# Zeroing the expert row table during the dense up stage, and forming the gate third of the last adaLN set behind the routing sums

## The chip, the cores and the metric

The kernel runs on one core of a Trainium2 chip. The metric is device time in microseconds (us), lower is better, taken as the median of several runs. The engines are TensorE (PE, with its weight loads as PEld), VectorE (DVE), ScalarE (ACT), GpSimd (POOL) and SyncE (SP), each with its own instruction queue; they meet only at semaphores. SP issues the weight loads, POOL issues the transfers of the expert rows, and all of them run on the same 16 DMA engines.

## The reference, cut to what matters

One inference step of a two-layer decoder on 256 prompt tokens and 8 sample tokens, width 1024, float32. Layer 1 ends in a mixture of experts behind an adaLN modulation:

```python
sh, sc, gt = ada_mod(c, ada_ffn_w[1], ada_ffn_b[1])    # (silu(c) @ w + b), split in three
hf = rms_norm(x, g_pre_ffn[1]) * (1.0 + sc) + sh
logits = hf @ w_router + b_router
top_v, top_i = lax.top_k(logits, 2); gates = softmax(top_v)
f = sum over e of dense_gate[:, e] * swiglu(hf, w1[e], w3[e], w2[e])
x = x + gt * rms_norm(f, g_post_ffn[1])
```

The thirds sh and sc of the set are needed before the router sees hf. The third gt is needed only for the last line.

## The kernel before

Tokens stand in columns (264 of them) and features in partitions, in 8 blocks of 128. Weights stream in as slabs of 1 MB through `ring`, which has 7 slots; SP issues the load of a slab when its slot is free. Every weight product but the adaLN ones is made in three passes over a high and a low part of the operands (lines 474 to 476): ACT writes the high part of a slab to `w_hi`, DVE the low part to `w_lo`.

**The adaLN sets.** Four sets, each 12 slabs of 4 x 128 rows and 512 columns, two slabs for each of 6 blocks `j` of columns. `ada_product(s, j)` (line 525) multiplies the nine conditioning vectors, which stand in columns 0 to 8 of `c32`, by two slabs; ACT copies the result (`ada_rows`, line 1015) to `arow`, and `ada_columns` (line 511) turns it into columns of bank 6, where DVE's `ada_take` (lines 1388 to 1391) adds the bias and folds the norm's gains in. Blocks 0 to 3 are sh and sc, blocks 4 and 5 are gt. A ring slot that holds an adaLN slab is free as soon as its product is done (`ada_used`).

**The last set and the routing**, the stage that the change touches, in the order of each engine:

- PE: the six products of set 3 with two norm sums in between (`norm_sum`, line 536), the logits (`logit_strips`, line 838: `c32` now holds the router's weights in columns 0 to 7), the transposes of hf to token rows (`token_rows`, line 846), the sum of the strips by `fold` (856), the positions in each expert (866), the loads (871), 8 triples of transposes of x (877), 8 transposes of the gate third (880), one count matmul (883), the gate rows spread over the tokens (888 and 889), the transposed picks (893), and then, once the rows of expert 0 are in (`x_in`) and the gate rows are out (`gate_taken`), the transposes of those rows (904) and the first expert.
- ACT: `ada_rows`, the norm's squares and roots, the router weights into `c32` (1251 and 1252), the high parts of the first three expert slabs (1262), the token rows out of PSUM (1268, 1269), the softmax exponent (1272), the rows of x out of PSUM (1276, 1277).
- DVE: the norm (1400, 1404), four small operations, `ada_take`, `modulate` (1413 to 1415), then the routing arithmetic up to the row numbers (1772), the gates, the picks (1797), and the gate rows (1801, 1806, 1807).
- POOL: after the output projection is out of PSUM (`wo_taken`) it sets `ye` to zero (1936) and writes it over the 8 slabs of the expert row table `x_rows` in DRAM (`clear`, 8 transfers of 512 KB, line 1945). Later it scatters the 264 token rows twice into that table (6 indirect transfers, 1950) and loads the slab of expert 0 (1986). Each expert takes 128 slots, so rows that no token fills have to be zero.
- SP: the 12 slabs of set 3 and behind them, without a break, those of expert 0. Expert slab k goes into the slot of adaLN slab 5 + k for k up to 6, and from slab 7 on a slot is free when DVE has written `w_lo` of the slab seven before.

Then 8 experts follow, 42 slabs each.

Of the kernel before, what the change touches and what calls it, by code (L numbers as in the profile page):

```python
# [12 lines left out]
P = 128  # L13
D = 1024
# [25 lines left out]
NEG = -1e30  # L40

# [56 lines left out]
def yoco_step(nc, w, o):  # L98
# [25 lines left out]
    with ExitStack() as ctx:  # L124
# [62 lines left out]
        rb = sb("rb", [NE, 1])  # L187
# [102 lines left out]
        rb_strip = at(11904, 1)  # L290
# [177 lines left out]
        def _(pe):  # L468
# [46 lines left out]
            def ada_product(s, j):  # L515
# [12 lines left out]
                if j >= 1:  # L528
                    ada_columns(s, j - 1)
# [294 lines left out]
            for j in range(6):  # L824
                ada_product(3, j)
                if j == 0:
                    norm_sum(5)
                if j == 2:
                    norm_sum(6)
            ada_columns(3, 5)  # L830


            def logit_strips(hf):

                pe.wait_ge(rw_spread, 1)
# [19 lines left out]
            for c, n in ((0, P), (1, P), (2, NB)):  # L855
                mm = pe.matmul(bank[0][0:n, NE * c:NE * (c + 1)], std[:, P * c:P * c + n], fold[:, 0:NE], start=True, stop=True)
# [15 lines left out]
            mm.then_inc(load_summed, 1)  # L872
            for k in range(KC):
                if k >= 2:
# [109 lines left out]
        def _(act):  # L984
# [128 lines left out]
            i_lin, i_wo = firsts[("wq", 0)], firsts[("wo", 0)]  # L1113
            highs(i_lin + 1)
# [127 lines left out]
            for j in range(6):  # L1242
# [30 lines left out]
            ins.then_inc(lg_exp, 1)  # L1273
            for k in range(KC):
# [66 lines left out]
        def _(dve):  # L1341
# [10 lines left out]
            dve.tensor_reduce(fold[:, :], ident.rearrange("p (a b) -> p b a", a=4)[:, 0:9, :], X, ALU.add).then_inc(fold_ready, 1)  # L1352
            dve.tensor_reduce(cst("head"), ident.rearrange("p (a r) -> p r a", a=8), X, ALU.add)
# [27 lines left out]
            def ada_take(s, kind, layer):  # L1381

                a = ada[:, s]
                dve.wait_ge(ada_turned, 6 * (s + 1))
# [3 lines left out]
                link(dve.tensor_tensor(a, sums, across(vec1[:, col:col + 24], 9), ALU.add))  # L1388
# [699 lines left out]
```

## Time and profile before

| | us |
|---|---|
| median of 3 runs (lowest, highest) | 1695.52 (1694.08, 1696.55) |
| span of the profiled execution | 1693.5 |
| busy: PE, PEld | 1587.1, 1295.9 |
| busy: DVE, ACT, POOL | 1255.3, 982.6, 153.9 |
| from the first product of set 3 to the first expert matmul | 638.55 to 713.13 |
| the 8 experts | 713.13 to 1672.8 |

The times are of whole executions. For the profiled execution only its span is given; the median of the runs is 2.0 us above that span, which is what lies around it. "Granted clock" in the tables of stretches is TensorE's clock as a share of 2.4 GHz: 0.50 is 1.2 GHz, 1.00 is 2.4 GHz, and a value between is a stretch in which it changed. A matmul of float32 shows as two instructions in the trace, so a product of 8 matmuls is "x16" there. Matmuls overlap, so the start of the next row says more than the length of one.

### The profile page before, as it was taken

How to read it: one execution, taken by the hardware profiler on the slowest of the kernel's cores; microseconds unless marked ns; L12 is line 12 of the kernel's file. 1: busy time of each engine (PE TensorE's matmuls, PEld its weight loads, DVE VectorE, ACT ScalarE, POOL GpSimd, SP SyncE). 2: the span in 40 equal slices, each digit the busy share in tenths (PEclk: the TensorE clock that was granted, in tenths of full speed). 3: DMA queues.
4: the chain of work that ended last, by engine and by line, in shares of the span. 5: the costliest groups of instructions: out<-in, count | busy, mean ns of one | idle time of the engine just before them, and what ended most of it. 6: DMA issues, size and time to landing. Idle time of an engine off the chain costs nothing.

```text
span 1693.5 us, 22933 instructions
## 1 busy us (share of the span) xinstructions
PE 1587.1 (94%) x8697; PEld 1295.9 (77%) x8697; DVE 1255.3 (74%) x1097; ACT 982.6 (58%) x885; POOL 153.9 (9%) x135
## 2 busy tenths in 40 slices
PE   6889999799899887899999999999999999999996
PEld 3579999498785574488888888888888888888874
DVE  4355543578782834488898888988888888889996
ACT  2244432433322633277777877877877877777774
POOL 0000000025541511200000000000000000000210
PEclk9789999899999988599999999999999999999998
DMA  9895555855458428689999999999999999999991
GB/s 345 295 346 177 180 160 183 299 174 194 155 212 305 141 75 333 214 320 382 359 389 384 355 395 364 380 387 379 370 391 367 378 386 364 382 386 363 394 386 49
DMA packets 248254, 512.28 MB, mean 302 GB/s; under 512 B 9046, under 2 KB 68614, under 8 KB 248176
## 3 DMA queue, kind: packets, MB, share of 16 engines
q1 hardware_dynamic: 241015, 490.27, 80.6%
q0 software_dynamic: 4768, 16.89, 2.5%
q10 hardware_dynamic: 2400, 4.17, 0.7%
q8 instruction: 45, 0.74, 0.2%
q14 instruction: 26, 0.21, 0.0%
HBM read 498.19 MB, written 13.82 MB: 302 GB/s over the span
## 4 chain that ended last, share of the span: by engine, by line
PE 76%; DVE 9%; DMA 5%; POOL 3%; ACT 3%; issue 3%; SPq 1%; DVEq 0%; ACTq 0%; POOLq 0%
PE wide L474 22%; PE wide L475 22%; PE wide L476 22%; DVE w_lo L1729 2%; POOL phase L1907 2%; DMA ring<-in_ada_mix_w 2%; DVE phase L1570 2%; DMA ring<-in_ada_ffn_w 1%; PE wide L930 1%; POOL phase L1913 1%; ACT w_hi L1262 1%; PE wide L525 1%; PE wide L536 1%; SPq L437 1%; DMA ring<-in_cache_v 1%
## 5 line engine op out<-in xcount | busy, mean ns | idle before, releaser
L1729 DVE TENSOR_TENSOR w_lo<-ring,w_hi 128x2048 fp32r<-128x2048 f32 x336 | 767.6, 2290 | 114.0 <-ACT w_hi L1262 112.5
L1262 ACT ACTIVATE w_hi<-ring 128x2048 fp32r<-128x2048 f32 x336 | 643.6, 1919 | 216.5 <-PE wide L476 214.3
L474 PE MATMUL wide<-w_hi,xe_hi 128*128 128x512 f32 x896 | 355.7, 397 | 5.6 <-DVE w_lo L1729 2.9
L475 PE MATMUL wide<-w_lo,xe_hi 128*128 128x512 f32 x896 | 350.2, 391 | 0.0
L476 PE MATMUL wide<-w_hi,xe_lo 128*128 128x512 f32 x896 | 350.2, 391 | 0.0
L474 PE MATMUL wide<-tHi,w_hi 128*128 128x264 f32 x672 | 198.3, 295 | 20.4 <-DVE mLo L1488 20.4
L404 DVE TENSOR_TENSOR w_lo<-ring,w_hi 128x2048 fp32r<-128x2048 f32 (+1 forms) x58 | 139.0, 2399 | 101.2 <-ACT w_hi L1002 100.9
L475 PE MATMUL wide<-mLo,w_hi 128*128 128x264 f32 x736 | 212.3, 288 | 0.0
L474 PEld LDWEIGHTS wide<-w_hi,xe_hi 128*128 128x128 f32 x896 | 169.0, 189 | 45.1 <-DVE w_lo L1729 8.6
L476 PEld LDWEIGHTS wide<-w_hi,xe_lo 128*128 128x128 f32 x896 | 168.8, 188 | 35.8
L475 PEld LDWEIGHTS wide<-w_lo,xe_hi 128*128 128x128 f32 x896 | 169.0, 189 | 33.4
L476 PE MATMUL wide<-tHi,w_lo 128*128 128x264 f32 x672 | 192.9, 287 | 0.0
L474 PE MATMUL wide<-w_hi,upT_hi 128*128 128x512 f32 x448 | 177.1, 395 | 0.0
L475 PE MATMUL wide<-w_lo,upT_hi 128*128 128x512 f32 x448 | 176.2, 393 | 0.0
L476 PE MATMUL wide<-w_hi,upT_lo 128*128 128x512 f32 x448 | 174.2, 389 | 0.0
L474 PEld LDWEIGHTS wide<-tHi,w_hi 128*128 128x128 f32 x672 | 129.3, 192 | 30.2 <-issue 29.9
L1002 ACT ACTIVATE w_hi<-ring 128x2048 fp32r<-128x2048 f32 (+1 forms) x58 | 109.1, 1885 | 61.2 <-PE wide L476 61.1
L475 PEld LDWEIGHTS wide<-mLo,w_hi 128*128 128x128 f32 x736 | 142.1, 193 | 0.3
L476 PEld LDWEIGHTS wide<-tHi,w_lo 128*128 128x128 f32 x672 | 129.0, 192 | 0.0
L476 PEld LDWEIGHTS wide<-w_hi,upT_lo 128*128 128x128 f32 x448 | 84.1, 188 | 19.0
L474 PEld LDWEIGHTS wide<-w_hi,upT_hi 128*128 128x128 f32 x448 | 84.1, 188 | 18.5
L475 PEld LDWEIGHTS wide<-w_lo,upT_hi 128*128 128x128 f32 x448 | 84.3, 188 | 16.5
(313 smaller groups left out, 1709.8 us busy)
## 6 DMA issues: line engine op xcount, KB each, us to landing
ring<-in_moe_w SPq DMA_DIRECT2D x336, 1024.0 KB, 7.4
ring<-in_ffn_w SPq DMA_DIRECT2D x30, 1024.0 KB, 5.4
ring<-in_ada_mix_w SPq DMA_DIRECT2D x24, 1024.0 KB, 8.8
ring<-in_ada_ffn_w SPq DMA_DIRECT2D x24, 1024.0 KB, 12.0
ring<-in_w_q SPq DMA_DIRECT2D x12, 1024.0 KB, 9.1
ring<-in_cache_k SPq DMA_DIRECT2D x24, 512.0 KB, 4.9
ring<-in_cache_v SPq DMA_DIRECT2D x24, 512.0 KB, 6.3
ring<-in_w_kv SPq DMA_DIRECT2D x8, 1024.0 KB, 6.5
```

Of the source, the lines that this page charges most:

```text
L404: eng.tensor_tensor(w_lo[:, i % PAIRS, 0:size], ring[:, n % RING, 0:size], w_hi[:, i % PAIRS, 0:size].bitcast(F32), ALU.subtract).then_inc ...
L437: sp.dma_start(slab_view(n), slab_source(item)).then_inc(slab_in[n % RING], 16)
L474: pe.matmul(out, a[0], b[0], start=start, stop=False, skip_group_check=True)
L475: pe.matmul(out, a[0], b[1], start=False, stop=False, skip_group_check=True)
L476: return pe.matmul(out, a[1], b[0], start=False, stop=stop, skip_group_check=True)
L525: mm = pe.matmul(out[32 * k:32 * (k + 1), :], c32[:, 4 * half + k, :], slab_view(n)[:, k, :], start=(half == 0), stop=(half == 1))
L536: mm = pe.matmul(bank[7][:, 0:NT], ones, tT[:, k, :], start=(k == 0), stop=(k == KC - 1))
L1002: act.activation(w_hi[:, i % PAIRS, 0:size], ring[:, n % RING, 0:size], ACT.Copy).then_inc(hi_done, 1)
L1262: act.activation(w_hi[:, (NSPLIT + k) % PAIRS, :], ring[:, slot, :], ACT.Copy).then_inc(hi_done, 1)
L1570: ins = dve.tensor_tensor(k_prod[t % 2][:, cols], slab_view(n)[:, t % 2, cols], bank[6 + q], ALU.mult)
L1729: dve.tensor_tensor(w_lo[:, i, :], ring[:, slot, :], w_hi[:, i, :].bitcast(F32), ALU.subtract).then_inc(lo_done, 1)
L1907: pool.tensor_tensor(out, rawT[:, r % 4, :], cos, ALU.mult).then_inc(cos_done, 1)
```

## The change

Two things are done, and a third follows from them.

1. **Zeroing.** POOL no longer waits for the output projection. Behind its three small loads in the up stage of the dense feed-forward (the router's weights and bias, and cos and sin) it waits until both halves of the operand's low part are written (`act_lo`), sets the first 1024 columns of `hT` to zero and issues the 8 transfers from there. DVE, before it writes `hT` again (`gated(1, mT)`), waits for all 8 to have landed.
2. **The gate third.** Of set 3, PE, ACT and DVE do blocks 0 to 3 in the old place. The products of blocks 4 and 5 stand behind the loads (line 879 and 880 of the new kernel), their columns behind the first two of the 8 triples of transposes of x, and DVE's share behind the picks. The count matmul moves ahead of the gate's transposes, because DVE writes the gate third only after the picks, which need the count.
3. **The router's weights** must now be in `c32` together with the conditioning vectors. They go to columns 16 to 23, once, right after set 2; `fold_r` is the sum matrix for those columns, and the router's bias stands in partitions 16 to 23 of `rb`, in place of `rb_strip`.

```diff
             pe.wait_ge(wo_taken, KC)
-            for j in range(6):
+            pe.wait_ge(rw_spread, 1)
+            for j in range(4):
                 ada_product(3, j)
...
-            ada_columns(3, 5)
+            ada_columns(3, 3)
...
             mm.then_inc(load_summed, 1)
+            pe.wait_ge(ht_taken, KC)
+            ada_product(3, 4, columns=False)
+            ada_product(3, 5, columns=False)
             for k in range(KC):
+                if k == 2:
+                    ada_columns(3, 4)
+                    ada_columns(3, 5)
                 if k >= 2:
                     pe.wait_ge(x2_taken, k - 1)
...
+            pe.wait_ge(arow_ready, 6 * 3 + 5)
+            pe.matmul(bank[2][:, 0:P], ones, before, start=True, stop=True).then_inc(count_row, 1)
+            pe.wait_ge(ada_taken, 5)
             for k in range(KC):
                 mm = pe.transpose(bank[6 + k // 4][0:1 + NB, P * (k % 4):P * (k % 4 + 1)], ada[:, 3, 16 + k, :], ident)
             mm.then_inc(gate_turned, 1)
-            pe.wait_ge(ht_taken, KC)
-            pe.matmul(bank[2][:, 0:P], ones, before, start=True, stop=True).then_inc(count_row, 1)
...
+            act.wait_ge(ada_used, 36)
+            act.wait_ge(in_router, 32)
+            act.activation(c32[:, :, ROUTER:ROUTER + NE], rw[:, :, :], ACT.Copy).then_inc(rw_spread, 1)
             highs(i_lin + 1)
...
-            for j in range(6):
+            for j in range(4):
                 ada_rows(3, j)
...
-            act.wait_ge(ada_used, 48)
-            act.wait_ge(in_router, 32)
-            act.activation(c32[:, :, 0:NE], rw[:, :, :], ACT.Copy)
-            act.activation(c32[:, :, NE:NE + 1], c32[:, :, NE + 1:NE + 2], ACT.Copy).then_inc(rw_spread, 1)
...
             ins.then_inc(lg_exp, 1)
+            ada_rows(3, 4)
+            ada_rows(3, 5)
...
+            dve.wait_ge(cleared, 16 * NE)
             gated(1, mT)
...
-            ada_take(3, 1, 1)
+            ada_take(3, 1, 1, 0, 16)
...
             ins.then_inc(pick_ready, 1)
+            ada_take(3, 1, 1, 16, 24)
             dve.wait_ge(gate_turned, 1)
...
             pool.wait_ge(in_rope, 16)
+            pool.wait_ge(act_lo, 2)
+            pool.memset(hflat[:, 0:D], 0.0).then_inc(zero_ready, 1)
+            pool.wait_ge(zero_ready, 1)
...
+            clear(0, hflat[:, 0:D])
...
-            pool.wait_ge(wo_taken, KC)
-            pool.memset(ye[:, :], 0.0).then_inc(zero_ready, 1)
-            pool.wait_ge(zero_ready, 1)
...
-            clear(0)
             pool.wait_ge(cleared, 16 * NE)
             pool.wait_ge(ht_taken, KC)
             pool.wait_ge(row_ready, 1)
```

**PE at the end of set 3**, before. A row is a line of the kernel, the operation, its output and inputs and the output's shape, and in brackets the semaphores that it waits for; L525 is a product, L511 the columns, L838 the logits:

```order
L511 MATMUL wide<-fold,shared 128x9 [waits arow_ready]
L511 MATMUL wide<-fold,shared 128x9 x3
L525 MATMUL wide<-ring,c_60 32x512 [waits slab_in2,arow_ready]
L525 MATMUL wide<-ring,c_60 32x512 x3
L525 MATMUL wide<-ring,c_60 32x512 [waits slab_in3]
L525 MATMUL wide<-ring,c_60 32x512 x3
L511 MATMUL wide<-fold,shared 128x9 [waits arow_ready]
L511 MATMUL wide<-fold,shared 128x9 x3
L511 MATMUL wide<-fold,shared 128x9 [waits arow_ready]
L511 MATMUL wide<-fold,shared 128x9 x3
L838 MATMUL wide<-hT,c_60 32x264 [waits h_ready,rw_spread]
```

and in the changed kernel, where the same lines are 526, 512 and 839:

```order
L526 MATMUL wide<-ring,c_60 32x512 [waits slab_in5,arow_ready]
L526 MATMUL wide<-ring,c_60 32x512 x3
L526 MATMUL wide<-ring,c_60 32x512 [waits slab_in6]
L526 MATMUL wide<-ring,c_60 32x512 x3
L512 MATMUL wide<-fold,shared 128x9 [waits arow_ready]
L512 MATMUL wide<-fold,shared 128x9 x3
L512 MATMUL wide<-fold,shared 128x9 [waits arow_ready]
L512 MATMUL wide<-fold,shared 128x9 x3
L839 MATMUL wide<-hT,c_60 32x264 [waits h_ready]
L839 MATMUL wide<-hT,c_60 32x264 x3
```

The logits stood behind six pairs of slabs and now stand behind four; the last pair ahead of them is the one in ring slots 5 and 6.

**PE behind the loads**, before (L871 are the loads, L877 the transposes of x, a triple for each block k):

```order
L871 MATMUL wide<-phase,const 128x8 x3
L877 MATMUL wide<-const,xT 128x128 x2
L877 MATMUL wide<-const,xT 8x128
L877 MATMUL wide<-const,xT 128x128 x2
L877 MATMUL wide<-const,xT 8x128
L877 MATMUL wide<-const,xT 128x128 [waits x2_taken]
```

and now, where L872 are the loads, L884 the transposes of x and L512 the columns:

```order
L872 MATMUL wide<-phase,const 128x8 x3
L526 MATMUL wide<-ring,c_60 32x512 [waits slab_in0,arow_ready,ht_taken]
L526 MATMUL wide<-ring,c_60 32x512 x3
L526 MATMUL wide<-ring,c_60 32x512 [waits slab_in1]
L526 MATMUL wide<-ring,c_60 32x512 x3
L526 MATMUL wide<-ring,c_60 32x512 [waits slab_in2,arow_ready]
L526 MATMUL wide<-ring,c_60 32x512 x3
L526 MATMUL wide<-ring,c_60 32x512 [waits slab_in3]
L526 MATMUL wide<-ring,c_60 32x512 x3
L884 MATMUL wide<-const,xT 128x128 x2
L884 MATMUL wide<-const,xT 8x128
L884 MATMUL wide<-const,xT 128x128 x2
```

Four groups of four matmuls of 512 columns stand between the loads and the transposes of x; the first waits for the token rows to be out of PSUM (`ht_taken`). The columns of both blocks come behind the second triple.

**PE at the gate's transposes**, before (L880), with the count matmul (L883) behind them:

```order
L877 MATMUL wide<-const,xT 8x128
L880 MATMUL wide<-const,ada 9x128 x8
L883 MATMUL wide<-const 128x128 [waits ht_taken]
L888 MATMUL wide<-phase,mT 128x512 [waits x2_taken,gate_rows]
L889 MATMUL wide<-phase,const 8x512
```

and now, count matmul L887, gate's transposes L890:

```order
L884 MATMUL wide<-const,xT 8x128
L887 MATMUL wide<-const 128x128 [waits arow_ready]
L890 MATMUL wide<-const,ada 9x128 [waits ada_taken]
L890 MATMUL wide<-const,ada 9x128 x7
L896 MATMUL wide<-phase,mT 128x512 [waits x2_taken,gate_rows]
L897 MATMUL wide<-phase,const 8x512
```

The gate's transposes now wait for `ada_taken`, that is for DVE, which does its share behind the picks, which wait for the count matmul.

## Rows read from the trace of the kernel before

**Rows 1.** Chain that ended last, 610 to 725 us: start, length, what.
```profile
649.89 16.98 DMA ring<-in_ada_ffn_w
673.25 1.38 DVE hT L1413 x4
697.43 6.94 DMA x_rows<-phase,row
704.66 3.72 DMA hT<-x_rows
708.51 1.96 PE wide L904 x8
713.13 0.79 PE wide L474
```

**Rows 2.** Page, costliest groups: busy, mean ns, idle before and its releaser.
```profile
L474 PE MATMUL wide<-w_hi,xe_hi 128*128 128x512 f32 x896 | 355.7, 397 | 5.6 <-DVE w_lo L1729 2.9
```

**Rows 3.** Instructions in order of time, PE, 656 to 669 us: start, length.
```profile
656.91 1.92 PE L525 MATMUL wide<-ring,c 128*32 128x512 f32 x16
658.76 1.06 PE L511 MATMUL wide<-fold,shared 128*128 128x9 f32 x8
...
666.92 1.83 PE L525 MATMUL wide<-ring,c 128*32 128x512 f32 x8 [1.55 <-DMA ring<-in_ada_ffn_w]
668.68 3.58 PE L511 MATMUL wide<-fold,shared 128*128 128x9 f32 x16
```

**Rows 4.** Instructions in order of time, DVE, 659 to 673 us.
```profile
659.37 2.55 DVE L1404 TENSOR_TENSOR tT<-xT,rstd 128x1056 f32<-128x1056 f32 x2
...
662.13 0.15 DVE L1721 TENSOR_SCALAR phase<-const 128x8 f32<-128x8 f32 x1
...
672.30 0.38 DVE L1388 TENSOR_TENSOR ada<-wide,vec 128x216 f32<-128x216 f32 x1 [9.72 <-PE wide L511]
```

**Rows 5.** Stretches: busy of each engine, then granted clock, DMA share, GB/s.
```profile
655.00:660.00 5.00, 5.00 (x36) 2.91 (x40) 2.44 (x2) 1.08 (x2) 0.00 (x0) 1.00 1.04 417
670.00:675.00 5.00, 2.27 (x11) 2.17 (x11) 2.43 (x9) 3.49 (x2) 0.00 (x0) 0.50 1.05 388
```

**Rows 6.** DMA queues, 639 to 658 us: POOL's queue, packets, MB, share.
```profile
q0 software_dynamic: 963, 3.55, 45.8%
```

**Rows 7.** Instructions in order of time, PE, 685 to 708 us.
```profile
686.89 1.54 PE L877 MATMUL wide<-const,xT 128*128 128x128 f32 x6
688.82 4.59 PE L877 MATMUL wide<-const,xT 128*128 128x128 f32 x18 [0.39 <-ACT phase L1277]
693.20 1.62 PE L880 MATMUL wide<-const,ada 128*9 128x128 f32 x8
694.66 0.39 PE L883 MATMUL wide<-const 128*128 128x128 f32 x2
697.45 1.75 PE L888 MATMUL wide<-phase,mT 9*128 9x512 f32 x2 [2.40 <-DVE phase L1801]
```

**Rows 8.** Instructions in order of time, DVE, 695 to 708 us.
```profile
695.16 1.04 DVE L1797 TENSOR_SCALAR phase<-wide,phase 128x128 f32<-128x128 f32 x3 [0.91 <-PE wide L883]
696.12 1.27 DVE L1801 COPY phase<-wide 9x512 f32<-9x512 f32 x2
704.83 0.69 DVE L1806 COPY phase<-wide 128x512 f32<-128x512 f32 x1 [7.44 <-PE wide L889]
...
706.64 0.67 DVE L1807 COPY phase<-wide 8x512 f32<-8x512 f32 x1
```

**Rows 9.** Stretches of 1 us in which TensorE's clock stands or changes.
```profile
694.00:695.00 1.00, 1.00 (x8) 0.67 (x5) 0.22 (x2) 0.00 (x0) 0.69 (x2) 0.80 1.00 270
...
718.00:719.00 1.00, 1.00 (x5) 0.86 (x4) 0.00 (x0) 0.36 (x1) 0.00 (x0) 0.86 0.00 0
```

**Rows 10.** Instructions in order of time, POOL, up stage: its last small load.
```profile
119.84 0.58 POOL L1900 DMA_DIRECT2D const<-in_shape_constants  x1
```

**Rows 11.** A stretch of the up stage, columns as in Rows 5.
```profile
132.00:134.00 2.00, 2.00 (x19) 2.00 (x18) 0.78 (x1) 0.00 (x0) 0.00 (x0) 1.00 0.21 42
```

More of the change, by code:

```diff
@@ L40 @@
 NEG = -1e30
+ROUTER = 16
 CONST = {}
@@ L513, in ada_columns, with ada_product @@
                 mm.then_inc(ada_turned, 1)
-            def ada_product(s, j):
+            def ada_product(s, j, columns=True):
                 if 6 * s + j >= 2:
@@ L527, in ada_product @@
                     mm.then_inc(ada_used, 1)
-                if j >= 1:
+                if j >= 1 and columns:
                     ada_columns(s, j - 1)
@@ L855, in _ @@
             for c, n in ((0, P), (1, P), (2, NB)):
-                mm = pe.matmul(bank[0][0:n, NE * c:NE * (c + 1)], std[:, P * c:P * c + n], fold[:, 0:NE], start=True, stop=True)
+                mm = pe.matmul(bank[0][0:n, NE * c:NE * (c + 1)], std[:, P * c:P * c + n], fold_r[:, :], start=True, stop=True)
             mm.then_inc(lg_summed, 1)
@@ L1379, in across, with ada_take @@
                 return a.unsqueeze(2).to_broadcast(list(a.shape[:2]) + [n])
-            def ada_take(s, kind, layer):
+            def ada_take(s, kind, layer, lo=0, hi=24):
                 a = ada[:, s]
-                dve.wait_ge(ada_turned, 6 * (s + 1))
+                dve.wait_ge(ada_turned, 6 * s + hi // 4)
                 dve.wait_ge(vec_read, 1)
@@ L1898, in _, with slab_rows, clear @@
             pool.dma_start(rw[:, :, :], w["router_w"][0].rearrange("(k p) n -> p k n", p=P)).then_inc(in_router, 16)
-            pool.dma_start(rb[:, :], w["router_b"].rearrange("a n -> n a")).then_inc(in_router, 16)
+            pool.dma_start(rb[ROUTER:ROUTER + NE, :], w["router_b"].rearrange("a n -> n a")).then_inc(in_router, 16)
             pool.dma_start(const[:, 0:2 * NT], w["shape_constants"][:, 0:2 * NT]).then_inc(in_rope, 16)
             pool.wait_ge(in_rope, 16)
+            pool.wait_ge(act_lo, 2)
+            pool.memset(hflat[:, 0:D], 0.0).then_inc(zero_ready, 1)
+            pool.wait_ge(zero_ready, 1)
+            def slab_rows(table, e, c):
+                at = SLOTS * (e + NE * max(c - 1, 0))
+                return table[min(c, 1)][at:at + SLOTS, :]
+            def clear(c, zeros):
+                for e in range(NE):
+                    pool.dma_start(slab_rows(x_rows, e, c), zeros).then_inc(cleared, 16)
+            clear(0, hflat[:, 0:D])
             def turned_half(r):
@@ L1934, in _ @@
             pool.sem_inc(y_free, 1)
-            pool.wait_ge(wo_taken, KC)
-            pool.memset(ye[:, :], 0.0).then_inc(zero_ready, 1)
-            pool.wait_ge(zero_ready, 1)
-            def slab_rows(table, e, c):
-                at = SLOTS * (e + NE * max(c - 1, 0))
-                return table[min(c, 1)][at:at + SLOTS, :]
-            def clear(c):
-                for e in range(NE):
-                    pool.dma_start(slab_rows(x_rows, e, c), ye[:, :]).then_inc(cleared, 16)
             def scatter(over):
```

22 lines of the change are left out of this document (12 added, 10 removed).

## The prediction, made before the changed kernel ran

> **What bounds the kernel now.** I read three views, in this order. The page says who is late in the experts, where most of the time goes: the 896 matmuls of line 474 waited 5.6 us in all [rows 2]. TensorE is the bound there, the change touches nothing in it, and so what counts is when the first expert starts. The chain of waits, followed back from that start, shows what held it: a weight slab of set 3 that took 16.98 us to land, then `modulate`, the routing, the scatter of the token rows, the gather of expert 0's rows (landed at 708.38), and the transposes of those at 708.51 [rows 1]. The instructions in order of time show who would be next: DVE had put the last gate row out at 707.31 [rows 8]. So the gate's chain was 1.1 us short of being the bound, and the rows have only this much to gain before it takes over, unless it moves too. That makes this stage a race of two chains, and the change hurries one and lengthens the other.
>
> **Part by part.** All times are in the profiled execution (span 1693.5 us); the median of the runs lies 2.0 us higher.
>
> *The head of the stage.* The product of block 3 began at 656.91, the last one, of block 5, got its second slab only at 666.92 [rows 3]. With the blocks 4 and 5 gone, columns of block 2 end at 659.8, ACT needs 0.6 us beside them, and the columns of block 3 take 1.06 [rows 3]: done at 660.9. DVE is later: the norm ends at 661.92, its small operations at 662.28 [rows 4]; two of them go, which saves 0.2. `ada_take` took 0.95 us from 672.30 to `modulate` at 673.25 [rows 1, 4]; without the gate third I take 0.75. So `modulate` starts at 662.4 + 0.75 = 663.15, **10.1 us earlier**. The new bound here is the norm, not the slabs. How much faster the slabs land without the 4.2 MB of zeros is then worth nothing by itself: slabs 6 and 7 were in time before, too. I let the routing behind it shift as it is: TensorE has a gap between 660.9 and the logits, which come behind the first half of `modulate`; behind the like gap before, its clock stood at 0.50 in 670 to 675 [rows 5], and I expect it at half in the routing again.
>
> *The scatter and the gather.* Shifted by 10.1, the last scatter lands at 694.3 and expert 0's rows allow the transposes at 698.4. That is the ceiling: a gain of 10.1.
>
> *The gate's chain.* Loads end and the transposes of x begin at 686.89 [rows 7], now 676.8. From there:
> - Products of blocks 4 and 5, new in this place: 8 matmuls took 1.83 us at half clock [rows 3] and 16 took 1.85 at full (656.91 to 658.76). All four groups: 7.3 at half, 3.7 at full. The clock rose 5.0 us after the first dense matmul at 713.13 [rows 1, 9]; taking that, 5.0 at half and the remaining 2.3 at full in 1.2: **6.2**, ends 683.0.
> - Two triples of x at full clock, half of the 1.54 that six matmuls took [rows 7]: 0.8. Two sets of columns: 3.58 at half, 1.06 each at full [rows 3]; I take 2.0, since the clock has just risen. ACT's two copies, 0.6 each, lie beside them. Ends 685.8.
> - Six triples: 4.6 as before [rows 7], since the columns are light work and I expect the clock to fall again. Ends 690.4.
> - Count matmul until the picks 0.5 (694.66 to 695.16), picks 0.96 [rows 7, 8]: 691.9. The picks were released by the count matmul, not by DVE's own work ahead of them [rows 8], and now the more so.
> - `ada_take` for the gate third, now between picks and gate rows: the 0.95 less its middle operation, 0.6. Ends 692.45. PE waits for it with nothing else to do.
> - Gate's transposes 1.46 (693.20 to 694.66) and 0.1 to DVE; gate rows 1.33 (696.12 to 697.45); spread 7.38 (697.45 to 704.83); out 2.48 and 0.1 to PE [rows 7, 8]. Together 12.85: **705.3**.
>
> Before, the transposes began at 708.51, so the gain is **3.2 us**. Of the 10.1 won, 6.9 are given back: the gate's chain, 20.4 us from the loads' end to 707.31, gets 8.0 longer (6.2 + 2.0 + 0.7 for DVE and its hop, less 1.1 on the first triples and the wait behind them), and it was 1.1 short of the rows.
>
> The clock is the soft term. After 688.82 this stretch had nothing but transposes, and the clock rose to full in 694 to 695 [rows 7, 9]. The Trainium skill, "TensorE: Matmul & The Clock Gate", Part 4, says that transposes do not count as activity for the clock; this trace speaks against it. By that rule the two triples behind the products would let the clock fall ahead of the columns.
>
> *The zeroing.* It adds a POOL memset of 1 us and 8 issues behind the load at 119.84 [rows 10]; nothing is queued behind them on POOL but the cosine products of the projection stage, behind the whole feed-forward. The 4.2 MB take 10 us of all DMA engines at 417 GB/s [rows 5]. In the up stage the DMA share was 0.21 in the 2 us from 132 while TensorE ran without a gap [rows 11]: a slab is 48 matmuls, at least 5 us by the 19 in 2 us, and 2.5 us of DMA, with seven slots to run ahead. I cost it at nothing. DVE's wait on `cleared` has the rest of the feed-forward, far over 10 us, to cover it.
>
> *Small pieces.* The router copy on ACT, one small operation, stands where ACT then waits for `modulate` of set 2; the two new DVE operations at the start are under a wait for weights. Nothing. Expert slabs 0 to 2 are asked for as before and have no zeros beside them, so ACT has their high parts no later, against the routing, than before. In the experts nothing changes if slabs 3 to 9 are there: they now wait for the products (slot free from 678.8 to 683), seven slabs and 2.16 MB of scatter are 9.5 MB, at 388 GB/s [rows 5] done by 703.2, ahead of the first expert matmul at 709.9.
>
> **The rivals.**
> - *The clock does not rise in the products* (or falls before the columns). For it: from 666.92 two groups' worth of work, a product and both columns, ran at half throughout [rows 3, 5]. Against: there the groups had a gap, here four stand back to back. Price: products +1.1, triples +0.7, columns +1.6: 3.4, start 708.7, 0.2 later than before: 1695.7.
> - *It rises and falls again under the two triples.* Then only the columns pay, 1.6: gain 1.6, 1693.9. For it: light work let it fall before; against it, the rise in 694 among transposes [rows 9]. This is the case that the rule above would give.
> - *The rows come late.* The scatter and gather now share the DMA with seven slabs, before with three. POOL's queue moved 3.55 MB in 19 us beside the slabs [rows 6], 187 GB/s, so 2.16 MB take 11.6 us and the 0.5 MB of the gather up to 2 us more than alone; I expect the rows at 700. At worst they wait until all is through: 703.2 + 3.72 [rows 1] = 706.9, gain 1.5: 1694.0.
> - *The clock is full in the spread.* Before, the clock rose in 694 and the spread began 2.8 us later, still mostly at half by its length [rows 7, 9]. At full the spread takes 3.7, the start is near 701, where the rows are: gain 7.5, 1688.0.
> - *Slower: the zeros starve the up stage.* If the ring has not caught up when they start, at about 122, the weights come 10.1 us late (4.2 MB), and TensorE, which is the bound there, waits. It decides once fewer than two slabs are ahead. 10.1 - 3.2: 1702.4. The row at 132 speaks against it.
> - *It does not do what it says:* the head is still bound by slabs. But both slabs of block 3 were there at 656.9 [rows 3]. Very unlikely, and counted with the last.
>
> **How the numbers follow.** Forecast 1695.5 - 3.2 = 1692.3, chance 0.62 with its own range 1690.5 to 1694. Clock does not rise 0.07 (1695.7), rises and falls again 0.08 (1693.9), rows late 0.05 (1694.0), clock full in the spread 0.12 (1688.0), slower 0.06 (1702.4). What a measurement of this kernel can tell from no change is about 0.2%, 3.4 us, and the forecast lies right at that edge: of its 0.62 I put 0.35 beyond 1692.1, since I took the triples and the gate's transposes at half clock. Faster by over 0.2%: 0.35 + 0.12 = 0.47; within: 0.27 + 0.07 + 0.08 + 0.05 = 0.47; slower 0.06. The range 1688.0 to 1696.5 leaves out the slower case and about half of the fastest.
>
> **What would show it.** `modulate` of set 3 near 663 and no DMA wait ahead of it; the four product groups in 6 to 7 us with the clock going from 0.50 to 1.00 among them; the first expert's transposes released by DVE's last gate row, not by the gather, with the gather landed 4 to 5 us earlier; the up stage of the same length. I am wrong if the gather releases the transposes, if the spread takes much less than 7.4 us, or if the first expert starts within 1 us of 708.5.

## The result, and the profile after

The changed kernel took 1706.21 us, median of 4 runs (1701.36 to 1707.18), against 1696.03 us (1694.08 to 1696.84): a ratio of 1.0052, 95% interval 1.0032 to 1.0072. It is slower by 10.2 us where 3.2 us less were forecast. The profiled execution has a span of 1704.2 us, 10.7 above that of before.

Four marks split those 10.7 us. The third row of the table is the stage that the prediction was about; it did better than forecast. The loss is in the experts, of which the prediction said that nothing changes there.

| us | before | after | difference |
|---|---|---|---|
| start to set 3's first product | 638.55 | 641.75 | +3.20 |
| from there to `modulate` of set 3 | 34.70 | 24.50 | -10.20 |
| from set 3's first product to the first expert matmul | 74.58 | 69.15 | -5.43 |
| first to last expert product | 958.44 | 972.19 | +13.75 |
| behind it | 21.93 | 21.11 | -0.82 |

The chain of waits of the changed kernel, from set 3 to the first expert (start, length, what); it answers to [rows 1]:

```profile
641.75 1.97 PE wide L526 x16
...
666.25 1.38 DVE hT L1426 x4
...
690.35 8.35 DMA x_rows<-phase,row
...
698.99 7.16 DMA hT<-x_rows
706.28 1.96 PE wide L912 x8
...
710.90 0.79 PE wide L475
```

The slab load of 16.98 us is gone from the chain, and `modulate` starts 24.5 us after set 3 and not 34.7. But the last scatter takes 8.35 us to land and the gather 7.16, where they took 6.94 and 3.72. The first expert's transposes are released by the gather.

The page's groups of the experts' products (busy us, mean ns of one, idle before and its releaser); the first answers to [rows 2]:

```profile
L475 PE MATMUL wide<-w_hi,xe_hi 128*128 128x512 f32 x896 | 360.3, 402 | 4.0 <-DVE xe_lo L1831 2.7
L476 PE MATMUL wide<-w_lo,xe_hi 128*128 128x512 f32 x896 | 354.7, 396 | 0.0
L477 PE MATMUL wide<-w_hi,xe_lo 128*128 128x512 f32 x896 | 354.7, 396 | 0.0
```

The first of them took 355.7 us before [rows 2], the other two:

```profile
L475 PE MATMUL wide<-w_lo,xe_hi 128*128 128x512 f32 x896 | 350.2, 391 | 0.0
L476 PE MATMUL wide<-w_hi,xe_lo 128*128 128x512 f32 x896 | 350.2, 391 | 0.0
```

So the three took 13.6 us less before, which is the loss in the experts. No wait has come in (idle 4.0 us against 5.6); each product has become 5 ns longer. The instructions in order of time show it as the distance from one start to the next. TensorE before, inside the third expert:

```profile
999.74 0.39 PE L474 MATMUL wide<-w_hi,xe_hi 128*128 128x512 f32 x1
999.97 0.39 PE L475 MATMUL wide<-w_lo,xe_hi 128*128 128x512 f32 x1
1000.20 0.39 PE L476 MATMUL wide<-w_hi,xe_lo 128*128 128x512 f32 x1
1000.42 0.39 PE L474 MATMUL wide<-w_hi,xe_hi 128*128 128x512 f32 x1
```

and after:

```profile
1001.35 0.39 PE L475 MATMUL wide<-w_hi,xe_hi 128*128 128x512 f32 x1
1001.58 0.40 PE L476 MATMUL wide<-w_lo,xe_hi 128*128 128x512 f32 x1
1001.82 0.39 PE L477 MATMUL wide<-w_hi,xe_lo 128*128 128x512 f32 x1
1002.05 0.40 PE L475 MATMUL wide<-w_hi,xe_hi 128*128 128x512 f32 x1
```

Three products take 0.68 us before and 0.70 after. Over some 2,500 steps between such products in the eight experts the mean is **227.3 ns before and 233.2 after**, at a granted clock of 1.00 in both. (The steps given below are such means; they resolve about 0.5 ns.) A row names the moving operand first (`w_hi`, 512 columns) and then the stationary one, which the weight load brings in (`xe_hi`, 128 by 128).

The cause, as the runs below show, is a line that the printed diff leaves out and the prediction passed over: `fold_r = sb("fold_r", [P, NE])` stands between `rb` and `flag`, ahead of `phase`. `sb` hands out SBUF in the order of its calls, in steps of 64 bytes per partition. So `flag` and `phase`, and with `phase` the tiles `xe_hi` and `xe_lo`, lie 64 bytes further on. No instruction of the experts' loop differs but in such addresses.

The 3.2 us ahead of set 3 are another thing. Stretches, with TensorE's busy time, granted clock, DMA share and GB/s, after:

```profile
550.00:555.00 5.00, 5.00 (x26) 0.60 1.10 348
555.00:560.00 5.00, 5.00 (x20) 0.50 1.06 383
```

and before:

```profile
550.00:555.00 5.00, 5.00 (x39) 1.00 1.10 349
555.00:560.00 5.00, 3.80 (x30) 1.00 1.06 383
```

In the prompt's attention the clock was at its lower level for some 10 us after, and not before. Ahead of that the two traces agree: the chain passes the same product of the query projection at 511.67 after and 511.84 before.

### The profile page after: what moved, and what is told of

The parts are those of the page before. It is cut to its first block, busy times and chain, and to the rows that moved or that the text cites. A ratio compares the mean times of both kernels' runs of the same rounds, so it can differ in the third digit from the quotient of the medians.

```text
span 1704.2 us, 22934 instructions
## 1 busy us (share of the span) xinstructions
PE 1603.5 (94%) x8697; PEld 1297.4 (76%) x8697; DVE 1254.9 (74%) x1098; ACT 982.1 (58%) x884; POOL 153.2 (9%) x135
## 4 chain that ended last, share of the span: by engine, by line
PE 78%; DVE 9%; DMA 3%; ACT 3%; issue 3%; POOL 3%; SPq 1%; DVEq 0%; ACTq 0%; POOLq 0%
PE wide L475 23%; PE wide L477 22%; PE wide L476 22%; DVE w_lo L1741 2%; DMA ring<-in_ada_mix_w 2%; PE wide L938 1%; POOL phase L1933 1%; DVE phase L1584 1%; PE wide L537 1%; ACT w_hi L1268 1%; PE wide L526 1%; SPq L438 1%; POOL phase L1939 1%; DMA ring<-in_cache_v 1%; DVE w_lo L405 1%
## 5 line engine op out<-in xcount | busy, mean ns | idle before, releaser
L475 PE MATMUL wide<-w_hi,xe_hi 128*128 128x512 f32 x896 | 360.3, 402 | 4.0 <-DVE xe_lo L1831 2.7
L476 PE MATMUL wide<-w_lo,xe_hi 128*128 128x512 f32 x896 | 354.7, 396 | 0.0
L477 PE MATMUL wide<-w_hi,xe_lo 128*128 128x512 f32 x896 | 354.7, 396 | 0.0
```

The lines of the kernel that those rows point to most:

```text
L475: pe.matmul(out, a[0], b[0], start=start, stop=False, skip_group_check=True)
L476: pe.matmul(out, a[0], b[1], start=False, stop=False, skip_group_check=True)
L477: return pe.matmul(out, a[1], b[0], start=False, stop=stop, skip_group_check=True)
```

## The experiments

Marks of the traces: the first product of set 3 (A), the first expert matmul counted from A (B), first to last expert product (C), and the mean step between products with `xe_hi` or `xe_lo`. Where there is one run, its time stands alone; the kernel before, run beside them, had medians of 1695.3 to 1696.5 us (1692.6 to 1700.6).

| kernel | us (runs) | A | B | C | step, ns |
|---|---|---|---|---|---|
| before | 1696.0 (4) | 638.55 | 74.58 | 958.44 | 227.3 |
| after | 1706.2 (4) | 641.75 | 69.15 | 972.19 | 233.2 |
| after_phase_at_old_place | 1689.9 (7) | 641.28 | 68.23 | 958.71 | 227.4 |
| before_phase_moved_64 | 1709.8 (4) | 637.23 | 74.31 | 972.77 | 233.2 |
| before_phase_moved_128 | 1710.6 (1) | 638.99 | 74.48 | 972.75 | 232.6 |
| before_phase_moved_256 | 1694.5 (1) | 637.53 | 74.21 | 958.58 | 227.4 |
| before_xe_and_behind_16 | 1714.5 (1) | 642.63 | 74.59 | 972.94 | 233.2 |
| before_behind_16 | 1696.7 (1) | 638.92 | 74.53 | 958.77 | 227.5 |
| before_xe_lo_and_behind_16 | 1701.0 (1) | 635.98 | 74.21 | 966.42 | 230.8 |
| before_w_hi_and_behind_64 | 1694.0 (1) | 636.35 | 74.44 | 958.83 | 227.4 |
| before_zero_early | 1689.3 (10) | 641.94 | 68.15 | 958.57 | 227.5 |
| after_gate_late_only | 1700.9 (7) | 639.75 | 76.77 | 957.93 | 227.5 |
| both_products_ahead_of_logits | 1689.6 (7) | 639.88 | 68.37 | 958.76 | 227.5 |
| products_and_columns_ahead | 1687.6 (5) | 639.79 | 67.53 | 958.71 | 227.5 |
| best_with_tT_moved_64 | 1687.4 (4) | 640.71 | 67.36 | 956.36 | 227.5 |

### Is it the place of `phase`?

**after_phase_at_old_place.**

```diff
-        fold_r = sb("fold_r", [P, NE])
         flag = sb("flag", [P, 1], I32)
         phase = sb("phase", [P, PHASE])
+        fold_r = sb("fold_r", [P, NE])
```

> The changed kernel with its new tile `fold_r` allocated behind `phase` and not ahead of it, so that `phase` and `flag` lie where they lay in the kernel before; no instruction differs but in an address. Theory P (place): the 64 bytes by which `fold_r` pushed `phase` cost about 6 ns on each of some 336 products of an expert whose stationary operand is `xe_hi` or `xe_lo` (both in `phase`), 14.6 us in eight experts, and perhaps the 3.2 us that the prompt's attention lost too (its q, k and scores lie in `phase`). Then 1706.2 - 14.6 = 1691.6 us, or 1688.4 with the 3.2; an expert takes 119.4 us, the products with `xe_hi` start 227 ns apart. Theory C (code): the loss comes with the program's instructions (fewer or more of them ahead of the experts' loop, other places of its code). Then 1706 us, an expert takes 121.3 us, steps of 233 ns.

Measured 1689.86 us, 0.9958 of before (0.9941 to 0.9976), steps of 227.4 ns. The page's groups, which stood at 360.3 and 354.7:

```profile
L475 PE MATMUL wide<-w_hi,xe_hi 128*128 128x512 f32 x896 | 356.6, 398 | 5.6 <-DVE w_lo L1741 2.9
L477 PE MATMUL wide<-w_hi,xe_lo 128*128 128x512 f32 x896 | 350.9, 392 | 0.0
L476 PE MATMUL wide<-w_lo,xe_hi 128*128 128x512 f32 x896 | 350.3, 391 | 0.0
```

One line in another place turns a change that is 10 us slower than before into one that is 6 us faster. A stayed late (641.28), so the 3.2 us are not of the place.

**before_phase_moved_64** is the reverse: the kernel before with an unused tile.

```diff
         rb = sb("rb", [NE, 1])
+        pad = sb("pad", [P, 16])
```

> The kernel before with an unused tile of 64 bytes per partition ahead of `flag` and `phase`. Theory P: 1696.0 + 14.6 to 17.8 = 1710.6 to 1713.8 us, an expert takes 121.3 us, and the last adaLN set starts 3.2 us later if that loss is of the place as well. Theory C: 1696.0 us, an expert takes 119.4 us.

Measured 1709.76 us, 1.0100 of before (1.0067 to 1.0133), steps of 233.2 ns, C longer by 14.3 us, A no later. The theory of the place holds both ways; the instructions of the change have no part in this loss.

### Which tile, and what has its place to agree with?

**before_xe_and_behind_16**: inside `phase`, everything from `xe_hi` on starts 16 elements later.

```diff
-        xe_hi = over("xe_hi", "phase", 8192, [P, KC, SLOTS], F32R)
-        xe_lo = over("xe_lo", "phase", 9216, [P, KC, SLOTS], F32R)
+        xe_hi = over("xe_hi", "phase", 8208, [P, KC, SLOTS], F32R)
+        xe_lo = over("xe_lo", "phase", 9232, [P, KC, SLOTS], F32R)
...
-        up_s = at(10240, 512)
+        up_s = at(10256, 512)
```

> The kernel before; `phase` stays, but inside it `xe_hi`, `xe_lo` and all that lies behind them (`grow`, `up_s`, `up`, the routing tables) start 16 elements (64 bytes) later. Theory P1, the place of the operand itself that TensorE loads as its stationary one: the products with `xe_hi` and `xe_lo` start 233 ns apart, as with `phase` moved, 1710 us. Theory P2, the place of the tiles that other engines read or write beside them (`up_s`, `up`): 1710 us too, the next kernel decides. Theory P3, something else in `phase` or `flag`: 227 ns, 1696 us.

**before_behind_16**, its control: the last pair of lines of that diff alone, and with it what lies behind `up_s`.

> The control to the one before it: only what lies behind `xe_lo` in `phase` (`grow`, `up_s`, `up`, the routing tables, from element 10240) starts 16 elements later; `xe_hi` and `xe_lo` stay. P1: steps of 227 ns, 1696 us. P2: steps of 233 ns, 1710 us. P3: 227 ns here and in the one before it.

Steps of 233.2 and 227.5 ns: it is `xe_hi` and `xe_lo` themselves (P1). The 1714.5 us hold an A of 642.6 as well, with the clock down at 550 here too.

**before_phase_moved_128** and **before_phase_moved_256** have `pad = sb("pad", [P, 32])` and `[P, 64]` in the place of the `[P, 16]` above:

> The kernel before with an unused tile of 128 bytes per partition ahead of `flag` and `phase`. If what decides is whether the stationary operand begins at a multiple of 128 bytes: 227 ns and 1696 us. If any distance from the old place costs (a multiple of 256 bytes or more is wanted): 233 ns and 1710 us.

> The kernel before with an unused tile of 256 bytes per partition ahead of `flag` and `phase`; 64 and 128 bytes made the experts' products start 233 ns apart. If the stationary operand wants a multiple of 256 bytes from the old place: 227 ns, 1696 us. If it is the distance to something else (`tT`, `w_hi`), or a wider step: 233 ns, 1710 us.

128 bytes cost as much as 64 (232.6 ns), 256 nothing (227.4). What counts repeats after 256 bytes, as far as these three distances tell.

The down products, whose operands (`w_hi`, `w_lo` and `upT_hi`, `upT_lo` in `tT`) did not move, changed too: their steps are 229.0 ns with `phase` at its old place, 229.6 with it 64 bytes further on (here and in the changed kernel), 231.2 with 128 and 229.0 again with 256. So the price is not confined to the products whose own operand moved. No run here tells why.

**before_xe_lo_and_behind_16**: the same diff without its lines on `xe_hi`.

> The kernel before; inside `phase` only `xe_lo` and what lies behind it start 64 bytes later, `xe_hi` stays. One product in three has `xe_lo` as its stationary operand. If each product pays by its own operand's place: two steps of three stay at 227 ns and one is longer, mean 229 ns, 1696.5 + 5 = 1701 us. If one shifted operand disturbs the pair: mean 233 ns, 1711 us; if only `xe_hi` matters: 227 ns, 1696.5 us.

Mean 230.8 ns. In order of time, TensorE:

```profile
1000.41 0.40 PE L476 MATMUL wide<-w_hi,xe_lo 128*128 128x512 f32 x1
1000.65 0.39 PE L474 MATMUL wide<-w_hi,xe_hi 128*128 128x512 f32 x1
1000.88 0.39 PE L475 MATMUL wide<-w_lo,xe_hi 128*128 128x512 f32 x1
1001.10 0.40 PE L476 MATMUL wide<-w_hi,xe_lo 128*128 128x512 f32 x1
```

Over all experts the step that begins with the product of `xe_lo` is 234.8 ns, the two others are 228.8 (`w_hi,xe_hi`) and 229.1 (`w_lo,xe_hi`). So some 7 of the 10 ns that three steps gain fall on the step of the moved operand's own product, nearest to the first of the three answers, and the rest on its neighbours: C is 8.0 us longer, more than the 5 expected. The weight load of `xe_lo` stands beside the product ahead of it:

```profile
1000.88 0.19 PEld L476 LDWEIGHTS wide<-w_hi,xe_lo 128*128 128x128 f32 x1
```

That is the step of 229.1 ns. The long step is the next one, in which TensorE multiplies with `xe_lo` and the load is that of `xe_hi`, at its old place.

**before_w_hi_and_behind_64** moves the moving operands along with all that lies behind them:

```diff
+        pad = sb("pad", [P, 16])
         w_hi = sb("w_hi", [P, PAIRS, SLAB], F32R)
```

> The kernel before with an unused tile of 64 bytes per partition ahead of `w_hi`, so that `w_hi`, `w_lo` (the moving operands) and all behind them, `tT` with `upT_hi` and `upT_lo` and `phase` with `xe_hi` and `xe_lo` too, lie 64 bytes later together. Modulo 256 the program's addresses before were 128 for `w_hi`, `w_lo`, `xe_hi`, `xe_lo` and 64 for `upT_hi` and `upT_lo`; here 192 and 128. Theory R (relative): a stationary operand is quick where it starts at the same place modulo 256 as the moving ones: the steps with `xe` stay at 227 ns, 1696 us. Theory A (absolute): it is quick at 128 modulo 256 itself: steps with `xe` 233 ns, those with `upT` fall from 229 to 227 ns: 1696 + 15 - 3 = 1708 us.

Steps of 227.4 ns with `xe`, 229.0 with `upT`, as before: theory R. It isn't the stationary operand's own address that counts but its distance to something that moved with it. Everything from `w_hi` on moved together here. `w_hi` and `w_lo` are what a product reads beside it, so they are the likeliest, but this run doesn't single them out. ACT and DVE write the same two tiles meanwhile; the traces show that the writes of neither are needed. Of the steps that lie wholly in a time with DVE at work and ACT idle, 233 before have a mean of 226.8 ns, and 228 after one of 232.3; with ACT at work and DVE idle it is 226.8 (193 steps) and 232.1 (243). With both idle there are too few to tell (1 and 4).

### What are the two parts of the change worth?

**before_zero_early**: the zeroing alone (the diff's hunks on `clear`, `zero_ready` and `cleared`), set 3 as before.

> The kernel before with the first part of the change alone: `x_rows` zeroed in the dense up stage from `hflat`, the wait ahead of the gated product of layer 1 too; set 3 of adaLN, `fold` and `rb` as before, and so `phase` at its old place. Theory P: no zero is in the way of the scatter, but the gate chain still ends at 708.5, so 1696.0 us within 1, an expert takes 119.4 us. Theory C, if it is GpSimd's code or the descriptors of the earlier zeroing that disturb the experts: up to 1706 us with steps of 233 ns.

1689.25 us, 0.9962 of before (0.9948 to 0.9977). I had expected no gain, and that was wrong. The chain:

```profile
666.05 1.85 PE wide L525 x16
667.91 1.90 PE wide L511 x16
...
670.77 1.38 DVE hT L1413 x4
...
694.78 6.61 DMA x_rows<-phase,row
...
701.68 3.66 DMA hT<-x_rows
705.47 1.95 PE wide L904 x8
```

The zeros (8 writes of 512 KB) had run beside the last slabs of set 3, one of which took 16.98 us [rows 1]. Without them no slab is late, all six products still stand ahead of `modulate`, and this starts 28.8 us after A and not 34.7: 5.9 us of the 10.2 are the zeroing's.

**after_gate_late_only**: the gate third behind the routing sums, the zeroing late as before, `phase` at its old place.

> The second part of the change alone, with `phase` at its old place: gate third of set 3 behind the routing sums, `x_rows` zeroed late from `ye` as before. Theory P: an expert takes 119.4 us; the start of the experts is between that of the whole change (710.9 - 3.2 = 707.7 with `phase` at its old place) and that of the kernel before (713.1): 1690 to 1696 us, nearer to 1691 if the eight zeroing writes end before the scatter wants its queue. Theory C: if the code of the second part does the harm, 1704 to 1710 us with steps of 233 ns.

1700.88 us, 1.0028 of before (1.0011 to 1.0045): slower, where 1690 to 1696 had been expected. The chain:

```profile
661.82 14.29 DMA ring<-in_moe_w
676.20 1.91 ACT w_hi L1268
...
697.15 7.62 DMA x_rows<-phase,row
...
705.05 6.72 DMA hT<-x_rows
711.90 1.95 PE wide L912 x8
```

`modulate` is early (24.5 us after A), but the expert slabs now come beside the zeros, one in 14.29 us; ACT waits for it before it turns to the token rows, and scatter and gather are slow as in the whole change. B is 2.2 us longer.

With the zeroing in place the gate's move is worth nothing: B is 68.15 with the zeroing alone and 68.23 with both, and the medians agree. It brings `modulate` forward by 4.3 us (28.8 to 24.5), and from there to the experts takes 4.4 us more (39.3 to 43.7). The lead lasts until the last scatter is issued, 47.9 us after A and not 52.8. Then the scatter takes 8.00 us and not 6.61, the gather 7.25 and not 3.66, and these 5.0 us use it up.

### Where does the gate's move lose its gain?

**both_products_ahead_of_logits**, from after_phase_at_old_place:

```diff
             ada_columns(3, 3)
+            ada_product(3, 4, columns=False)
+            ada_product(3, 5, columns=False)
...
             logit_strips(0)
+            pe.wait_ge(arow_ready, 6 * 3 + 6)
             token_rows(0)
...
             mm.then_inc(load_summed, 1)
             pe.wait_ge(ht_taken, KC)
-            ada_product(3, 4, columns=False)
-            ada_product(3, 5, columns=False)
```

ACT's two `ada_rows` move with them.

> The changed kernel with `phase` at its old place, and the products (3, 4) and (3, 5) of the gate third issued right behind the columns of product (3, 3), where TensorE waited 4.2 us for `hT` (idle ahead of the logits' first matmul at 667.59); their columns stay behind the routing sums. Theory D (the loads collide): the two products hold four slots of the ring until 682.4, so the expert slabs' loads stood still from 668.5 to 682.5 and then ran at some 410 GB/s beside scatter and gather, which took 8.0 and 7.25 us where the zeroing alone had 6.6 and 3.7. Here the slots come free at 667, the loads end by some 687, scatter and gather take about 6.6 and 3.7: first expert product 4.5 to 5 us earlier (504.9 us after 200 of the chain, that is at about 704.7 and not 709.5), 1685 us. Rival E: scatter and gather are slow for a reason of their own (nearer to the scores, the gather's rows): first expert product at 709.5 still, 1690 us. Rival F: the products delay the logits by 1.5 us or more and the clock falls: 1691 us or more.

(The numbers in the middle of that are garbled; what is meant is a first expert product at 704.7.) Measured 1689.55 us. Stretches of after_phase_at_old_place (busy time of each engine, then clock, DMA share and GB/s):

```profile
668.00:682.00 14.00, 13.18 (x96) 6.46 (x88) 10.83 (x36) 8.27 (x22) 1.63 (x1) 0.79 0.15 45
682.00:690.00 8.00, 5.84 (x47) 4.30 (x44) 5.19 (x17) 4.28 (x17) 6.48 (x6) 1.00 1.01 340
690.00:704.00 14.00, 7.60 (x19) 1.96 (x19) 3.75 (x6) 0.39 (x1) 0.72 (x2) 0.66 1.04 411
```

and the instructions of the new kernel, TensorE:

```profile
679.71 1.54 PE L885 MATMUL wide<-const,xT 128*128 128x128 f32 x6
681.04 3.42 PE L512 MATMUL wide<-fold,shared 128*128 128x9 f32 x16
684.31 4.56 PE L885 MATMUL wide<-const,xT 128*128 128x128 f32 x18
...
693.37 2.07 PE L897 MATMUL wide<-phase,mT 9*128 9x512 f32 x2 [1.37 <-DVE phase L1815]
...
703.60 1.97 PE L913 MATMUL wide<-const,hT 128*128 128x128 f32 x8 [1.74 <-DVE phase L1821]
```

In the upper fence the DMA engines all but stand still for 14 us (share 0.15), while the slabs of the two products hold four slots of the ring, and then run full under scatter and gather. The same stretches with the products ahead:

```profile
668.00:682.00 14.00, 10.52 (x62) 8.67 (x62) 8.42 (x31) 10.48 (x27) 0.59 (x1) 0.67 0.86 306
690.00:704.00 14.00, 9.93 (x21) 2.69 (x22) 4.56 (x10) 0.39 (x1) 1.50 (x2) 0.61 0.56 221
```

With the products ahead, the gather issued at 697.26 landed in 3.6 us and not in 7.25, the last scatter in 6.7 and not in 8.0. So the collision (theory D) is real. But the end did not move: the transposes are now released by DVE's last gate row, 2.7 us after the rows are in. The clock had fallen by 674 and stood at 0.50 until 689, and the gate's chain ran at half: six triples 4.6 us, columns 3.4. Theory D was right about the transfers. Rival F was right about the clock but not about its reason: the logits were not delayed (they start 26.3 us after A in both kernels). Together the two cancel.

**products_and_columns_ahead**, on top of that:

```diff
             logit_strips(1)
+            ada_columns(3, 4)
+            ada_columns(3, 5)
             token_rows(2)
...
             for k in range(KC):
-                if k == 2:
-                    ada_columns(3, 4)
-                    ada_columns(3, 5)
```

> The kernel with both products ahead of the logits, and besides the two sets of columns (3, 4) and (3, 5) (3.2 us at half clock, at 681.25 to 684.46 there) issued ahead of `token_rows(2)`, where TensorE waited 3.4 us for ScalarE. There the rows had landed by about 701.0 and TensorE turned them at 703.60 because the gate chain ended last. If that reading holds, the gate chain ends 3 us earlier, the rows bound again at about 701.1, and the first expert product starts 65.9 us after set 3's first product and not 68.4: 1687 us. If the gate chain loses the 3 us again (the clock falls earlier), 1689.5.

1687.64 us, 0.9952 of before (0.9933 to 0.9971), B 67.5: 0.8 us better where 2.5 were expected. The gate's chain still ends last:

```profile
689.04 1.88 PE L890 MATMUL wide<-const,ada 128*9 128x128 f32 x8 [2.58 <-DVEq L1405]
692.28 2.07 PE L896 MATMUL wide<-phase,mT 9*128 9x512 f32 x2 [1.37 <-DVE phase L1814]
```

The gate's transposes now take 1.88 at half clock, where after_phase_at_old_place had 1.04 at full, and TensorE waits 2.58 us for DVE ahead of them: the chain runs through DVE's `w_lo` work for the first expert (two of them, 4.40 us, from 681.31).

**best_with_tT_moved_64**, on top of that: `upT_hi` and `upT_lo` stand to `w_hi` as `xe_hi` does.

```diff
+        pad = sb("pad", [P, 16])
         tT = sb("tT", [P, KC, NT])
...
         rb = sb("rb", [P, 1])
+        pad2 = sb("pad2", [P, 48])
         flag = sb("flag", [P, 1], I32)
```

> The kernel with products and columns ahead, with 64 unused bytes ahead of `tT` and 192 more ahead of `flag` and `phase`, so that `upT_hi` and `upT_lo` start at 128 modulo 256, as `w_hi`, `w_lo`, `xe_hi` and `xe_lo` do (64 before). By both theories of the place the 168 down products of an expert, 229 ns apart now, come to 227: 8 x 168 x 2 ns = 2.7 us less, 1685 us. If the down products don't care: 1687.6 us. If other stages suffer (`tT` is a moving operand of the dense stages as `tHi`): more.

The steps between down products fell from 229.0 to 227.0 ns, and C from 958.71 to 956.36, 2.4 us, near the 2.7 expected. Modulo 256, `upT` has changed its place against `w_hi` and `w_lo`, and `xe` has not. From the page, before this edit and with it:

```profile
L475 PE MATMUL wide<-w_hi,upT_hi 128*128 128x512 f32 x448 | 177.0, 395 | 0.0
L476 PE MATMUL wide<-w_lo,upT_hi 128*128 128x512 f32 x448 | 176.0, 393 | 0.0
```

```profile
L477 PE MATMUL wide<-w_hi,upT_hi 128*128 128x512 f32 x448 | 175.7, 392 | 0.0
L478 PE MATMUL wide<-w_lo,upT_hi 128*128 128x512 f32 x448 | 174.4, 389 | 0.0
```

The median of 1687.37 us (0.9954, 0.9937 to 0.9970) doesn't resolve that against 1687.64. It is the lowest median of the kernels with several runs, 8.9 us below the kernel before and 18.8 below the changed one. Against the zeroing alone (1689.25, with runs from 1685.7 to 1694.7) it isn't shown to be faster.

### The 3.2 us ahead of set 3

The clock had been down at 550 in all six traces with the early zeroing and in two of nine without it. Four repeats, without any edit of their own: **before_again_1** and **before_again_2**, **zero_early_again_1** and **zero_early_again_2**.

> The kernel before, unchanged, once more, for one question: TensorE's granted clock fell to 0.50 between 550 and 560 in all six profiles of kernels with the early zeroing and in two of nine without it, and set 3 began about 2.5 us later in these. If it is chance in each execution, some of these two and the two of the zeroing alone fall in either kind: dips mixed, first product of set 3 at 636 to 643 in both. If the early zeroing brings it: none here (set 3 at 636 to 640).

> The kernel before with the early zeroing alone, once more. If the early zeroing brings the fall of the clock at 550: a fall in both repeats, set 3 at 640 to 642. If it is chance: one of the two without it is to be expected.

> The kernel before, unchanged, a second repeat. No fall at 550 if the early zeroing brings it, a fall in some of the repeats if it is chance.

> The zeroing alone, a second repeat. A fall at 550 here too if the early zeroing brings it; if it is chance, one of its two repeats without it is to be expected.

None of the four shows it. The zeroing alone, first repeat:

```profile
550.00:555.00 5.00, 5.00 (x41) 1.00 1.10 348
555.00:560.00 5.00, 3.36 (x26) 1.00 1.07 387
```

A was 637.49 and 638.32 in the kernel before (1694.86 and 1695.58 us), 638.05 and 636.86 with the zeroing (1688.53 and 1687.55 us). So the zeroing does not bring the fall with it each time. It follows on a stretch (540 to 546) in which TensorE waited for the cache's slabs, busy down to 1.35 us of each 2; executions without the fall have that stretch as well. The fall comes in some executions of either kind: in 6 of 8 traces with the early zeroing and in 2 of 11 without. Where it came, A was 639.75 to 642.63, elsewhere 635.98 to 638.99. Whether it is likelier with the zeroing stays open; that much of the profiled execution's 3.2 us can be chance is shown, since A spans 3.0 us without any fall.

## Why the prediction was wrong, point by point

**In the experts nothing changes: false, and nearly the whole error.** This is the step that failed: a term put at nothing. It looked at waits, slots and slabs alone, and the first paragraph said of TensorE there that the change touches nothing in it. It touches where the stationary operand lies: a step between products went from 227.3 to 233.2 ns, 13.75 us over eight experts. The profiled execution lies 13.9 us above the forecast in all; the other differences (3.2 ahead of set 3, 2.2 less in the stage, 0.8 less behind the experts) nearly cancel. With the place undone, the time is 1689.9 us, inside the stated range of 1688.0 to 1696.5, but a gain of some 6 us and not 3.2. No rival had it: the slower one was the zeros in the up stage, which did not occur.

**`modulate` 10.1 us earlier, bound by the norm: right**, 10.2 measured from A. That the faster slabs were then worth nothing by themselves was right only with the gate third gone; alone, the zeroing was worth 5.9 us, and a sum for each part by itself would have asked what it does.

**The gate's chain ends at 705.3: too late.** It ended at 705.69, or 702.5 with the 3.2 us of A taken off. The terms, predicted and measured: products 6.2 and 5.7 (679.80 to 685.51), two triples 0.8 and 0.7, columns 2.0 and 1.7, six triples 4.6 and 3.1, count and picks 1.46 and 1.46, `ada_take` 0.6 and 0.6, gate's transposes 1.56 and 1.08, spread 7.38 and 7.71. The clock rose in the products as forecast, but did not fall in the six triples behind the columns. This was called the soft term, and with the gate's transposes, at full clock too, it was off by 2.0 us of the 2.8. (The forecast's list of what makes the gate's chain 8.0 us longer adds up to 7.8; the forecast itself doesn't hang on that.)

**The rows at 700: too early.** The transposes were released by the gather, at 706.28, or 703.1 without A's shift. This is the rival "the rows come late" (0.05), short of its worst case of 706.9. I had seen that seven slabs would now run beside the scatter, and by a mean rate I allowed 1.6 us for it: rows at 700 and not at the shifted 698.4, in which the last scatter and the gather keep their 6.94 and 3.72 us. They took 8.35 and 7.16, 4.9 us more. Both chains ended within 0.5 us of each other, at 705.69 and 706.15, so the stage gained 5.4 us and not 3.2: by luck, since one chain was over-priced and the other under-priced.

**The zeroing costs nothing in the up stage: right.** The chain passes the end of it and the query projection within 0.2 us of before.

**What would show me wrong** was named as the gather releasing the transposes, and it did; but the test that mattered, the mean of a product in the experts, was not on the list.

## What to carry to other kernels

When a diff adds or resizes a tile, list which tiles move behind it, and count that as a part of the change: put new small tiles behind the operands of the hot loop, or keep the stationary and the moving operands of that loop at one place modulo 256 bytes, which was the quickest of the places tried here. Where the page's mean of a matmul group changes by a few ns with no new wait, look at addresses before looking at the schedule. And price each part of a change alone: here one part gave all of the gain, and the other paid back its 4.3 us through loads that it held up and let go again beside the transfers that the next stage waited for.

## What the runs showed of the hardware

- A stationary operand of 128 by 128, with a moving one of 512 columns (both float32r, one instruction each), at a granted clock of 1.00: products start 227.4 ns apart when the stationary operand's address less that of `w_hi` is a multiple of 256 bytes, 233.2 ns at 64 bytes more, 232.6 at 128 more. At 64 less (`upT`) it is 229.0, and 227.0 once that is put right; but with `xe` at 128 more the steps of `upT` are 231.2 with `upT` unmoved. The weight load's own time is 188 to 189 ns in each. The 233.2 are a mean of two lengths that mostly take turns, about 231.5 and 235.2 ns.
- The Trainium skill, "TensorE: Matmul & The Clock Gate", Part 2, says that loading the next tile's weights takes no read bandwidth from the running matmul. The runs show that the place of the operands costs 6 ns of each step, but not that it is these two reads that meet: with `xe_lo` alone moved, the step beside its load is 229.1 ns and the one after it 234.8.
- The gather of 512 KB landed in 3.7 us where the slabs' loads were through (before_zero_early), and in 7.2 where seven of them still ran and the DMA engines moved 410 GB/s.
- TensorE's clock rose in the products of the changed kernel (0.92 in 684 to 685) and stayed at its upper level through six triples of transposes (687.93 to 691.05) and the gate's transposes. With products and columns earlier (products_and_columns_ahead) it was at the lower one through most of the triples, rose at 685 to 686 among transposes, and was down again in the gate's transposes at 689.04.
